# Second expert layer: the normed rows are copied into PSUM, and the dots read them there

## The reference, cut to what matters

```python
def peer(h, w_q, sub_keys, u_tab, v_tab):
    ...                                    # scores of 2 x 128 sub-keys for each of 8 heads
    best_s, best_pos = lax.top_k(cand_s, PEER_TOPK)          # 16 experts a head: 128 a token
    experts = jnp.take_along_axis(cand_i, best_pos, axis=-1)
    gates = jax.nn.softmax(best_s, axis=-1)
    ...
        u = u_tab[e_b]                                       # 128 rows of 1024 for each token
        act = jax.nn.gelu(jnp.einsum('td,thkd->thk', x_b, u))
        return jnp.einsum('thk,thkd->td', g_b * act, v_tab[e_b])
```

## Time and profile before

| | us |
|---|---|
| median of 3 runs | 5041.35 (5031.24 to 5054.4) |
| the profiled execution, its own time | 5044.04 |
| its span (first to last instruction) | 5041.9 |
| busy: PE / DVE / ACT / POOL | 3840.2 / 2578.8 / 975.3 / 2614.1 |
| dots (L1585) x1152, both layers | 1380.1 busy, 992.9 idle before them |
| `u` gathers on POOL x1152 | 1227.7 busy, mean 1066 ns |
| `v` gathers on POOL x1152 | 1334.8 busy, mean 1159 ns |
| moved by the gathers' queue | 1208.11 MB, 62.8% of 16 DMA engines |

### The profile page before, as it was taken

How to read it: one execution, slowest core, us unless ns; L and a number is a source line. 1 busy time by engine, 2 the same in 40 slices (tenths; PEclk the granted TensorE clock), 3 DMA queues, 4 the chain that set the end, 5 groups by cost and what they waited for, 6 DMA issues and landing times. The chain is left out here.

```text
span 5041.9 us, 41707 instructions
## 1 busy us (share of the span) xinstructions
PE 3840.2 (76%) x11081; PEld 1863.9 (37%) x11081; DVE 2578.8 (51%) x6419; ACT 975.3 (19%) x2603; POOL 2614.1 (52%) x2407
## 2 busy tenths in 40 slices
PE   2377885999999999677768777856677677676776
PEld 0144543454444444343214543432233233232322
DVE  1115347665665665467421551575545545555543
ACT  0012111334333333111110220111111111111111
POOL 0010001777767777677740000017777877777775
PEclk8689887999999999898879557878888788888888
DMA  9400023999999999999980001229999999999998
GB/s 346 170 6 0 34 64 118 397 372 389 383 356 380 389 365 365 381 371 343 398 308 41 5 15 58 60 69 373 351 394 368 346 394 362 355 393 365 364 394 317
DMA packets 509377, 1381.48 MB, mean 274 GB/s; under 512 B 84466, under 2 KB 176691, under 8 KB 508276
## 3 DMA queue, kind: packets, MB, share of 16 engines
q0 software_dynamic: 331776, 1208.11, 62.8%
q1 hardware_dynamic: 176996, 170.89, 10.6%
q10 hardware_dynamic: 432, 0.44, 0.0%
HBM read 1374.86 MB, written 6.09 MB: 274 GB/s over the span
## 5 line engine op out<-in xcount | busy, mean ns | idle before, releaser
L1585 DVE SCALAR_TENSOR_TENSOR px_rows<-px_rows,h 128x1024 f32<-128x1024 f32 x1152 | 1380.1, 1224 | 992.9 <-DMA px_rows<-in_peer_u,px_experts 978.0
L1880 PE MATMUL bank<-px_rows,px_d 128*128 128x512 f32 (+1 forms) x2304 | 1322.6, 658 | 642.4 <-DMA px_rows<-in_peer_v,px_experts 616.3
L1554 POOL DMA_INDIRECT px_rows<-in_peer_u,px_experts x1152 | 1227.7, 1066 | 784.7 <-DVE px_experts L1629 401.6
L1554 POOL DMA_INDIRECT px_rows<-in_peer_v,px_experts x1152 | 1334.8, 1159 | 415.5 <-issue 309.5
L1881 PE MATMUL bank<-px_rows,px_d 128*128 128x512 f32 (+1 forms) x2304 | 1264.8, 632 | 0.0
L1880 PEld LDWEIGHTS bank<-px_rows,px_d 128*128 128x128 f32 (+1 forms) x2304 | 435.9, 202 | 1210.6 <-issue 1095.2
L1881 PEld LDWEIGHTS bank<-px_rows,px_d 128*128 128x128 f32 (+1 forms) x2304 | 459.8, 200 | 643.6 <-issue 643.6
L1784 ACT ACTIVATE px_d<-ident,px_coef 128x128 f32<-128x128 f32 x1024 | 344.5, 391 | 1107.9 <-DVE px_coef L1595 1085.3
L1386 PE MATMUL bank<-pk_hT,pk_w 128*128 128x512 f32 x512 | 229.9, 603 | 0.0
L1666 DVE TENSOR_REDUCE px_ntop<-bank 128x1 f32<-128x512 f32 (+1 forms) x72 | 46.0, 639 | 322.3 <-PE bank L1903 321.9
L1386 PEld LDWEIGHTS bank<-pk_hT,pk_w 128*128 128x128 f32 x512 | 96.8, 194 | 110.6 <-issue 110.6
(11 more groups left out here) (350 smaller groups left out, 4031.9 us busy)
## 6 DMA issues: line engine op xcount, KB each, us to landing
mr_w<-in_w_mod SPq DMA_DIRECT2D x24, 2048.0 KB, 20.1
px_room<-in_cache_mla_ckv SPq DMA_DIRECT2D x256, 128.0 KB, 5.8
px_rows<-in_peer_u,px_experts POOLq DMA_INDIRECT x1152, 6.8
px_rows<-in_peer_v,px_experts POOLq DMA_INDIRECT x1152, 6.6
pk_w<-in_peer_w_q SPq DMA_DIRECT2D x32, 512.0 KB, 3.7
px_room<-in_peer_w_q SPq DMA_DIRECT2D x16, 512.0 KB, 14.2
mod_prompt<-mod_rows SPq DMA_DIRECT2D x4, 1536.0 KB, 6.4
sp_w<-in_swa_w_qkv SPq DMA_DIRECT2D x1, 6144.0 KB, 19.8
```

The lines of the kernel that those rows point to most:

```text
L1554: pool.indirect_dma_start(row_buf[n % RING][:], None, table, offset(ap=experts[:, slot:slot + 1], axis=0)).then_inc(landed[n % RING], 16)
L1585: nc.vector.scalar_tensor_tensor(out=u[:], in0=u[:], scalar=1.0, in1=h2[:, tile_of(slot), :], op0=ALU.mult, op1=ALU.mult, accum_out=dots[: ...
L1880: pe.matmul(bank[0][0:m, :], d[:, 0:m], v[:, 0:512], start=first, stop=last)
```

## The change

The eight PSUM banks become slices of one PSUM tensor, so that two neighbouring banks can be read as one row of 1024 columns. In layer two, ScalarE copies a tile's `h2` into banks 2 and 3 (even tiles) or 4 and 5 (odd tiles), 512 columns a copy: tiles 0 and 1 ahead of everything else, tile t + 1 at slot 12 of tile t, once all dots of tile t - 1 are done. The dots of layer two take their second operand there; the first dot of a tile waits for the copy. Layer one reads `h2` in SBUF as before. The arguments that pass `psum` on are left out here.

```diff
-        bank = [ctx.enter_context(nc.psum_tensor(f"bank{i}", [P, 512], F32)) for i in range(8)]
+        psum = ctx.enter_context(nc.psum_tensor("bank", [P, 8, 512], F32))
+        bank = [psum[:, i, :] for i in range(8)]
...
+    wide = [psum[:, 2 + 2 * i:4 + 2 * i, :].rearrange("p b n -> p (b n)") for i in range(2)]
+    S_wide = sem(tag + "h_wide")
...
             def dot(slot):
                 dve.wait_ge(landed[u_th(slot) % RING], landings(u_th(slot)))
-                u = row_buf[u_th(slot) % RING]
-                nc.vector.scalar_tensor_tensor(out=u[:], in0=u[:], scalar=1.0, in1=h2[:, tile_of(slot), :], op0=ALU.mult, op1=ALU.mult,
+                u, t = row_buf[u_th(slot) % RING], tile_of(slot)
+                if latent is None and slot % HK == 0:
+                    dve.wait_ge(S_wide, t + 1)
+                h = wide[t % 2] if latent is None else h2[:, t, :]
+                nc.vector.scalar_tensor_tensor(out=u[:], in0=u[:], scalar=1.0, in1=h, op0=ALU.mult, op1=ALU.mult,
                                                accum_out=dots[:, slot % KEEP:slot % KEEP + 1]).then_inc(S_uf, 1)
...
+            def widen(t):
+                if t >= 2:
+                    act.wait_ge(S_uf, HK * (t - 1))
+                nc.scalar.copy(wide[t % 2][:, 0:512], h2[:, t, 0:512])
+                nc.scalar.copy(wide[t % 2][:, 512:D], h2[:, t, 512:D]).then_inc(S_wide, 1)
+
+            if latent is None:
+                widen(0)
+                widen(1)
             exps(0)
...
+                if latent is None and 1 <= t <= NTP - 1 and at == 12:
+                    widen(t + 1)
```

More of the change, by code:

```diff
@@ L153, in build @@
         renew_semaphores()
-        peer(nc, a, sbuf, sem, bank, x, ident, mod, mod_rows, stat, rstd, junk, 0, landed, latent)
+        peer(nc, a, sbuf, sem, bank, x, ident, mod, mod_rows, stat, rstd, junk, 0, landed, psum, latent)
         kept.close()
@@ L162, in build @@
             load_modulation(nc, sem, mod, mod_rows, 3)
-            peer(nc, a, sbuf, sem, bank, x, ident, mod, mod_rows, stat, rstd, junk, 1, landed, None)
+            peer(nc, a, sbuf, sem, bank, x, ident, mod, mod_rows, stat, rstd, junk, 1, landed, psum, None)
             final_norm(nc, a, o, sbuf, sem, x, stat, rstd, junk, tiles)
@@ L1224, in swa_sample, with peer @@
     s.close()
-def peer(nc, a, sbuf, sem, bank, x, ident, mod, mod_rows, stat, rstd, junk, layer, landed, latent):
+def peer(nc, a, sbuf, sem, bank, x, ident, mod, mod_rows, stat, rstd, junk, layer, landed, psum, latent):
     s = ExitStack()
@@ L1239, in peer @@
     peer_keys(nc, a, sbuf, sem, bank, x, ident, mod, stat, rstd, junk, n_tiles, layer, h2, best, key, ranks)
-    peer_rows(nc, a, sbuf, sem, bank, x, ident, mod, junk, stat, layer, h2, best, key, ranks, mod_rows, landed, latent)
+    peer_rows(nc, a, sbuf, sem, bank, x, ident, mod, junk, stat, layer, h2, best, key, ranks, mod_rows, landed, psum, latent)
     s.close()
@@ L1409, in peer_keys, with peer_rows @@
     s.close()
-def peer_rows(nc, a, sbuf, sem, bank, x, ident, mod, junk, stat, layer, h2, best, key, ranks, mod_rows, landed, latent=None):
+def peer_rows(nc, a, sbuf, sem, bank, x, ident, mod, junk, stat, layer, h2, best, key, ranks, mod_rows, landed, psum, latent=None):
     tag = f"px{layer}_"
```

## The result

The median after the change is 4905.85 us (4904.04 to 4908.72, 4 runs) against 5041.12 us (5031.24 to 5054.4, 4 runs): a ratio of 0.9727, 95% interval 0.9711 to 0.9744, 135.3 us less. The forecast was 4916 us, range 4880 to 4970. The profiled execution of the new kernel took 4905.43 us, its span is 4903.6 us.

The account below looks back on a forecast made before the run. POOL, its gathers held by layer two's dots, was taken as the bound, then the transfers: 145 us at most less 20 of holes gives 125, so 5044.0 - 125 = 4919 profiled, median 4916 us, range 4880 to 4970.

Parts of the forecast that it names:

- The lock on POOL: Layer two: dots with two SBUF operands hold POOL's gathers; one operand in PSUM gives POOL back 165 us.
- Rival (d): Layer two: the dot still holds POOL wherever its second operand lies, or its in-place write does; 5041 us, chance 0.06.
- the probe that was weighed in the prediction: Skill's probe: a copy stalled GpSimd-issued DMAs, tensor_tensor and tensor_reduce did not; by it the change gives 0 us.
- The transfers next: Layer two: transfers bind next, 1152 at 1.282 us need 1476 us against POOL's 1455; gain 145 us at most.
- Rival (c): Layer two: POOL is the bound and transfers follow at 415 GB/s; 165 us gained, 4876 us, chance 0.05.
- Rival (e): Layer two: transfers can't follow, 409 GB/s being a matter of the rows drawn; 5030 to 5041 us, chance 0.04.
- The holes: Layer two's four rank steps: VectorE's key-number work leaves transfers idle 5 us a step, 20 us in all.
- Rival (b): Layer two: the rank steps lie bare, 55 us in place of 20; 4951 us, chance 0.10.
- What was added: Layer two: dot at 1.24 us, ten ScalarE copies at 0.6 us each, VectorE's waits for copies; taken as costing nothing.
- rival (f): Layer two: TensorE left at 1.2 GHz for many slots becomes the bound; slower, 5145 us, chance 0.03.

Follow-up runs that it names:

- copies_only: Changed kernel with the copies into PSUM and their waits kept, but the dots reading h2 in SBUF again: 5041.01 us.
- the pair of extra sums: Changed kernel plus a 512-column sum after each layer-two dot: one operand in PSUM, 4924.81 us; both in SBUF, 5047.56 us.
- half_before: Kernel before the change, with layer two's gathers fetching only 512 columns of a row, of another expert: 5093.9 us, ratio 1.0105.
- swapped: Changed kernel with the dot's operands exchanged, PSUM first and gathered rows second: 4907.0 us.
- half_after: Changed kernel, with layer two's gathers fetching only 512 columns of a row, of another expert: 4888.67 us.

## Why the prediction was right

**The lock on POOL: right, and shown.** The step gave POOL 165 us back; its gathers' busy time fell by 166.6 us (from 679.6 + 584.0 with the five gathers missing from the earlier trace rows at their mean, 1268.8, to 1102.2). The means of 0.954 and 0.960 answer to 0.95 and 0.98. That this was what set the stage's end is shown by copies_only and by the pair of extra sums, and by half_before from the other side. Rival (d), that the dot holds POOL wherever its operand lies, is out by every gather like that at 4103.09; its doubt on the order of the operands by swapped.

The Trainium skill, "SBUF — State Buffer", Who interferes with whom, has beside the probe that was weighed in the prediction a rule that a VectorE instruction with two SBUF inputs contends with a GpSimd instruction that reads SBUF, and one with at most one SBUF input, outside the modes that use two ports, does not. The extra sums agree, 123 us apart. The probe's finding that `tensor_tensor` stalled nothing does not hold for these gathers (2.52 us at 3925.64, inside a tensor-tensor). The prediction weighed the probe alone, though the rule beside it speaks for its first step.

**The transfers next: right, and shown.** 1.282 us a gather against POOL's 1.24 was the step; the stage moves 405 GB/s or more in 67 of its 73 slices, POOL now waits 83 us for buffers, and half_after gains 17 us by halving the bytes. Rival (c), POOL as the bound at 4876, would have shown POOL without such waits, as half_after does. Rival (e), transfers that can't follow, is out with 406 GB/s over 1487 us. The other rule weighed, of the Trainium skill, "SBUF — State Buffer", A bandwidth-pool intuition that's wrong, gives about 358 GB/s from HBM to a core. The trace does not agree: the whole stage moved 406 GB/s, 13% more.

**The holes: the term that was mis-sized.** 20 us were taken for the four rank steps (bounds 0 to 55). Measured are 1492.3 - 1480.4 = 11.9 us, and the rank steps have 10.1 of them. The six slow slices are 41, 48, 18, 52, 27 and 20 GB/s short of 409, 206 x 20 us / 409 = 10.1 us; the rest lies at the stage's ends. The working counted VectorE's block of 13.7 us against the buffers, and took the transfers queued ahead as spent. They are not: a gather now lands 10.9 us after its issue, against 6.5, so by an estimate some eight (10.9 / 1.282) are under way at once where it was five (6.5 / 1.406). At 3933.53 POOL has waited 5.37 us for the dot behind the key numbers, and the slice around it still moves 361 GB/s. That this queue is what covers the block is read from these rows; no run changed it alone. The forecast for the profiled execution, 4919 us, lay 13.6 us above the measured 4905.43: some 8 us of it are these holes, and 5.7 the earlier start of the stage, which is chance and was no term of the sum. Rival (b), with the block bare at 55 us, is out.

**What was added: right.** The dot took 1219 ns against 1.24 us taken; the copies 581 ns against 0.6 us, and copies_only shows that they lie beside other work. VectorE's wait for a copy does not show among its waits, and rival (f) did not come: TensorE was granted 0.86 in the stage, busy for 1136 of 1487 us.

The miss of the study is not in the prediction but in its experiments: the price of a lock was carried to other patterns (half of the dots, an extra sum) by the number of locking instructions, and to another stage by the busy time that it would give back.

## What to carry to other kernels

When the queue of gathers looks full, compare the rate with its best stretch and the issuing engine's own instruction with its shortest one: a gather of 1.18 us beside others of 0.94 says that something holds the issuer, and the instruction that it starts inside says what. One of two SBUF operands moved to PSUM takes that hold away at no cost to VectorE. Then look for what is late next before doing the same elsewhere: it paid 135 us where POOL waited 12.8 us in all, 21 where it already waited 111 us for buffers, and nothing that showed where the transfers were full.

## What the runs showed of the hardware that was not expected

- What comes first decides who waits, and the two waits are not alike. In the kernel before, a gather that starts together with a dot is not held, and the dot is longer instead (below); one that starts 0.06 us into a dot is held, 1.97 us.

```profile
3617.15 1.26 DVE L1585 SCALAR_TENSOR_TENSOR px_rows<-px_rows,h 128x1024 f32<-128x1024 f32 x1
3617.15 0.93 POOL L1554 DMA_INDIRECT px_rows<-in_peer_v,px_experts  x1 [0.30 <-issue]
```

  In that profile 33 gathers start in the first 0.04 us of a dot and take 0.94 us. The dots' median is 1.225 us and their longest 1.296; with one operand in PSUM these are 1.220 and 1.223. So the dot loses 0.07 us at most, where the gather of the earlier trace rows lost 1.03.
- A held gather ends 0.80 to 0.82 us after the dot. So only about the first 0.12 us of its 0.94 can be held (an estimate from these durations). One that is past them goes on beside a dot untouched: 15 gathers that start 0.04 to 0.14 us ahead of a dot take 0.94 us.
- The hold's sum does not follow the locking time: 188 us from 690 us of dots, 161 with half of these dots, 194 with 394 us of sums, and 240 with all dots and half of the bytes, where a free gather takes 0.946 us. It depends on when in the instruction the gathers start (above); what sets that was not settled.
- VectorE takes 1024 columns with one operand in PSUM in the time that it takes from SBUF alone (1219 and 1226 ns), and 512 columns in exactly the same (684 ns both).
- One core's gathers of 4 KB rows kept 409 GB/s for most of 1480 us, beside a share of 1.02.
